# Nine odd merge gates computed in a stage of their own, four pairs of them by seven products, in a hybrid encoder layer

## The reference, cut to what matters

```python
h = rms_norm(x, pre_g); u = h @ w_in          # 1024 tokens x 1024
...                                           # ya, yb, yc: three attention branches, 1024 x 512 each
gates = jax.nn.sigmoid(mg).reshape(b, s, 3, D_MODEL)      # mg: the last 3*1024 columns of u
m = gates[:, :, 0] * (ya @ wa) + gates[:, :, 1] * (yb @ wb) + gates[:, :, 2] * (yc @ wc)
x = x + rms_norm(m @ w_out, post_g)
x = x + jax.nn.sigmoid(x @ w_pg) * (p_i @ w_pe)
```

## Time and profile before

| what | value |
|---|---|
| median of 3 runs | 1332.03 us (1331.99 to 1332.58) |
| the profiled execution: span from first to last instruction | 1330.3 us |
| the runs' median less that span (what lies around it) | 1.7 us |
| PE busy | 1312.1 us, 99% |
| DVE, ACT, POOL busy | 680.8, 575.5, 352.0 us |
| DMA | 72.18 MB, mean 54 GB/s |
| the chain that ended last | PE 90%, DVE 4%, ACT 3% |

### The profile page before, as it was taken

One profiled execution on the slowest core, in us unless ns is written; L12 is line 12 of the kernel. 1 busy time (PEld: TensorE's weight loads), 2 busy tenths in 40 slices (PEclk: granted clock), 3 DMA queues, 4 the chain that ended last, 5 costly groups with the idle time before them and its releaser, 6 DMA issues.

```text
span 1330.3 us, 17488 instructions
## 1 busy us (share of the span) xinstructions
PE 1312.1 (99%) x6636; PEld 1072.0 (81%) x6636; DVE 680.8 (51%) x1285; ACT 575.5 (43%) x1106; POOL 352.0 (26%) x239
## 2 busy tenths in 40 slices
PE   8999999999999999999999999999999999999998
PEld 6788877888888778788888888888877888888887
DVE  6354655556522677786633435555557337435222
ACT  6355455553222577676422245555554223223210
POOL 4122212222434311130244512221211443213100
PEclk9999999999999999999999999999999999999999
DMA  6111112111111200000111211111001114422111
GB/s 214 63 41 41 46 36 57 52 32 52 49 48 32 67 30 16 17 20 21 52 52 32 81 61 33 51 51 42 32 24 41 48 40 167 140 81 70 58 40 40
DMA packets 25712, 72.18 MB, mean 54 GB/s; under 512 B 2808, under 2 KB 4728, under 8 KB 25504
## 3 DMA queue, kind: packets, MB, share of 16 engines
q1 hardware_dynamic: 25632, 71.09, 16.9%
HBM read 66.86 MB, written 4.23 MB: 53 GB/s over the span
## 4 chain that ended last, share of the span: by engine, by line
PE 90%; DVE 4%; ACT 3%; issue 1%; DMA 1%; POOL 1%; SPq 0%; ACTq 0%; DVEq 0%; POOLq 0%
PE ps L934 18%; PE ps L953 14%; PE ps L1290 13%; PE ps L1548 7%; PE ps L1528 6%; PE ps L1175 5%; PE ps L1342 5%; PE ps L1331 2%; PE ps L973 2%; PE ps L1112 2%; PE ps L1028 2%; PE ps L1260 2%; PE ps L1554 2%; PE ps L1406 2%; PE ps L1143 1%; PE ps L1234 1%
## 5 line engine op out<-in xcount | busy, mean ns | idle before, releaser
L728 POOL TENSOR_TENSOR w_lo<-stage,w_hi 128x1024 fp32r<-128x1024 f32 (+2 forms) x84 | 190.3, 2265 | 577.5 <-ACT w_hi L1598 577.5
L1598 ACT CAST w_hi<-stage 128x1024 fp32r<-128x1024 f32 (+2 forms) x92 | 91.3, 992 | 198.0 <-PE ps L934 125.9
L2148 DVE TENSOR_TENSOR pt_lo<-ps,pt_hi 128x512 fp32r<-128x512 f32 (+2 forms) x160 | 97.1, 607 | 80.6 <-ACT pt_hi L1962 40.3
L953 PE MATMUL ps<-h_hi,w_hi 128*128 128x512 f32 x272 | 110.3, 405 | 0.0
L934 PE MATMUL ps<-h_hi,w_hi 128*128 128x512 f32 x352 | 108.9, 391 | 0.7 <-POOL w_lo L728 0.7
L934 PE MATMUL ps<-h_lo,w_hi 128*128 128x512 f32 x352 | 108.5, 389 | 0.0
L934 PE MATMUL ps<-h_hi,w_lo 128*128 128x512 f32 x352 | 108.4, 389 | 0.0
L1290 PE MATMUL ps<-h_hi,w_hi 128*128 128x512 f32 x256 | 106.8, 417 | 0.0
L953 PE MATMUL ps<-h_hi,w_lo 128*128 128x512 f32 x272 | 106.2, 391 | 0.0
L953 PE MATMUL ps<-h_lo,w_hi 128*128 128x512 f32 x272 | 106.1, 390 | 0.0
L1290 PE MATMUL ps<-h_hi,w_lo 128*128 128x512 f32 x256 | 100.5, 392 | 0.0
(11 more groups left out here) (386 smaller groups left out, 3059.3 us busy)
## 6 DMA issues: line engine op xcount, KB each, us to landing
stage<-in_w_gates SPq DMA_DIRECT2D x24, 512.0 KB, 3.6
stage<-in_w_qkvg_a SPq DMA_DIRECT2D x19, 512.0 KB, 4.4
stage<-in_w_qkvg_c SPq DMA_DIRECT2D x16, 512.0 KB, 3.6
m<-in_x_tok SPq DMA_DIRECT2D x8, 512.0 KB, 6.4
stage<-in_w_branch SPq DMA_DIRECT2D x8, 512.0 KB, 3.7
y_plain<-in_x_tok SPq DMA_DIRECT2D x8, 512.0 KB, 3.7
stage<-in_w_pg SPq DMA_DIRECT2D x16, 256.0 KB, 3.0
out<-y_plain SPq DMA_DIRECT2D x16, 256.0 KB, 2.0
```

The lines of the kernel that those rows point to most:

```text
L728: nc.gpsimd.tensor_tensor(dst, stage[:, staged, 0:width], f32(hi), ALU.subtract).then_inc(w_ready, 1)
L953: done = mm(ps[:, half_bank(T), :], w[:, slot, k * P:(k + 1) * P], h[:, k, g * SEQ:(g + 1) * SEQ], start=k == 0 and part == 0, stop=k == K ...
L1598: nc.scalar.copy(dst, stage[:, staged, 0:width]).then_inc(w_hi_done, 1)
L2148: sub = lambda out, whole, hi: nc.vector.tensor_tensor(out, whole, f32(hi), ALU.subtract)
```

## The change

Of the 24 gates the nine with f odd and at least 3 are taken out of the merges (gates 3, 5, 7 of each). They are computed right behind the first q and k, when h is ready. Gate (b=0, f=3) is plain (`plain_gate`, 24 matmuls for each group); the other eight go in four pairs J, each by seven products of 12 matmuls (`gate_product`). Pairs of gates are products of h by two weight blocks, so the state quarters and their sums are the same for all J and are formed once: POOL and DVE add hi and lo back together (four quarters of 128x2048), DVE forms four sums, ACT casts and DVE splits them. For each J, DVE forms four sums of weights and makes all the low parts, DVE does seven adds on PSUM, ACT takes tanh and SP stores each 128x512 quarter to DRAM (`gate_scratch`). In the merges SP reads the finished rows back into `s_row(1)` (`load_gate_row`).

In a merge PE now runs: gate 0, gate 1, branch 0, branch 1, gate 2, then for each pair: pair_first, pair_rest, gate 2p+2 (the gate of the pair behind it). In merge 2 both gates 4 and 6 stand behind pair 1, and branch 6 follows pair 2 directly. ACT, POOL, DVE and SP follow that order; numbers of weight blocks (`N_MERGE`, `N_B`, ...) and slots shift.

```diff
+GATE_PLAIN = (0, 3)
+GATE_PAIRS = [((0, 5), (0, 7)), ((1, 3), (1, 5)), ((1, 7), (2, 3)), ((2, 5), (2, 7))]
...
             def merge_gate(b, f, n, slot, c):
 
-                pe.wait_ge(mg_tanh, LEAD + b * KC + f - 1)
+                if c:
+                    pe.wait_ge(merged, LEAD + b * KC + 2)
+                else:
+                    pe.wait_ge(mg_tanh, LEAD + gate_tanhs(b, f - 2))
                 project(n, slot, gate_bank(b, c))
...
             def merge_rest(b):
 
-                n, slot = N_MERGE[b], N_MERGE[b] % 2
-                merge_gate(b, 2, n + 3, 1 - slot, 0)
-                merge_branch(b, 1, n + 4, slot)
-                merge_gate(b, 3, n + 5, 1 - slot, 1)
+                n = N_MERGE[b]
+                merge_branch(b, 1, n + 3, (n + 1) % 2)
+                merge_gate(b, 2, n + 4, n % 2, 0)
                 for p in PAIRS[b]:
...
+                    pair_first(b, p, at, at % 2)
+                    pair_rest(b, p, at + 1, 1 - at % 2)
+                    for c, number in enumerate(gates_behind(b, p)):
+                        merge_gate(b, 2 * p + 2 + 2 * c, number, number % 2, c)
                 if KC // 2 - 1 not in PAIRS[b]:
-                    merge_branch(b, 6, n + 14, slot)
-                    merge_branch(b, 7, n + 15, 1 - slot)
+                    merge_branch(b, 6, n + 11, (n + 11) % 2)
+                    merge_branch(b, 7, n + 12, (n + 12) % 2, count=2)
...
+            plain_gate(0)
             first_product("q", 1, range(KC))
             first_product("k", 1, range(KC))
+            plain_gate(1)
+            for J in range(N_PAIRS):
+                for product in range(7):
+                    gate_product(J, product)
+            pe.wait_ge(g_added, 7 * N_PAIRS - 4)
             half_step(-2, lambda T: None)
...
+            def gate_product(J, product):
...
+                gate_bank_free(7 * J + product)
+                if product == P1:
+                    pe.wait_ge(gw_ready, 4 * J + 2)
+                elif product == P3:
+                    pe.wait_ge(gw_ready, 4 * J + 3)
+                elif product == P7:
+                    pe.wait_ge(gw_ready, 4 * J + 4)
+                if J == 0 and product >= P6:
+                    pe.wait_ge(gt_ready, T_LO.index(state) + 1)
...
+            pool.wait_ge(h_ready, LEAD + QT)
+            for T, half in ((1, 0), (4, 1)):
+                hi, lo = h_quarter(half, 0)
+                nc.gpsimd.tensor_tensor(G_SUM[T], f32(hi), f32(lo), ALU.add).then_inc(gt_whole, 1)
```

More of the change, by code:

```diff
@@ new lines, in merge_rest, with plain_gate @@
+                if KC // 2 - 1 not in PAIRS[b]:
+                    merge_branch(b, 6, n + 11, (n + 11) % 2)
+                    merge_branch(b, 7, n + 12, (n + 12) % 2, count=2)
+            def plain_gate(g):
+                hi, lo = G_PLAIN
+                pe.wait_ge(gp_ready, 1)
+                if g == 0:
+                    pe.wait_ge(h_ready, LEAD + 6)
+                bank = [0, 3][g]
+                for k in range(KC):
+                    for part, (w, h) in enumerate([(hi, h_hi), (hi, h_lo), (lo, h_hi)]):
+                        done = mm(ps[:, bank, :], w[:, k * P:(k + 1) * P], h[:, k, g * SEQ:(g + 1) * SEQ],
+                                  start=k == 0 and part == 0, stop=k == KC - 1 and part == 2)
+                done.then_inc(gate_half, 1)
@@ new lines, in gate_product @@
+            def gate_product(J, product):
+                a, a22 = G_A1, G_A22[J % 2]
+                (s2s4, s3s1) = G_S
+                (hi, lo), first, state = {P1: (a, 0, "11"), P2: (a, SEQ, "21"), P3: (s2s4, SEQ, "22"), P6: (s2s4, 0, 2),
+                                          P7: (s3s1, 0, 3), P5: (s3s1, SEQ, 1), P4: (a22, 0, 4)}[product]
+                gate_bank_free(7 * J + product)
+                if product == P1:
+                    pe.wait_ge(gw_ready, 4 * J + 2)
[5 more added lines that the diff above has]
+                    pe.wait_ge(gt_ready, T_LO.index(state) + 1)
+                for c in range(QT):
+                    cols = slice(first + c * P, first + (c + 1) * P)
+                    for part, (w, h) in enumerate([(hi, 0), (hi, 1), (lo, 0)]):
+                        done = mm(ps[:, g_bank(J, product), :], w[:, cols], G_STATE[state][h][:, c, :],
+                                  start=c == 0 and part == 0, stop=c == QT - 1 and part == 2)
+                done.then_inc(g_done, 1)
@@ new lines, in merge, with plain_gate_hi @@
+                    split(n + 11, width=512)
+                    beside(range(2, 4))
+                    split(n + 12, width=512, count=2)
+                    act.wait_ge(block_done, LEAD + n + 9)
+                    act.wait_ge(merged, LEAD + b * KC + 5)
+                    nc.scalar.activation(s_row(0), banks(gate_bank(b, 1)), ACT.Tanh, scale=0.5).then_inc(mg_tanh, 1)
+            def plain_gate_hi():
+                act.wait_ge(gp_in, 16)
+                nc.scalar.copy(G_PLAIN[0], stage[:, 0, :]).then_inc(gw_hi_done, 1)
@@ L2383, in merge @@
                     state_lo(j)
[L2384 removed]
+                merge_add(b, 1, n + 3, 1)
                 state_lo(3)
```

569 lines of the change are left out of this document (409 added, 160 removed).

## The result

| | before | changed |
|---|---|---|
| median of 12 runs | 1332.08 us | 1335.63 us |
| ratio, 95% interval | | 1.0024 (1.0016 to 1.0032) |
| span of the profiled execution | 1330.3 us | 1334.4 us |

The changed kernel is slower: by 0.24% in the ratio, which is estimated from all runs, and by 3.6 us (0.27%) between the medians. The prediction had 6.8 us more, 1338.8, and a range of 1331.5 to 1346.0: the sign, the range and the places are right, the size is twice what came.

What follows compares the result with a forecast made beforehand. PE's matmul count times start spacing was taken as the bound. Terms -10.9 - 0.5 + 2.7 + 0.4 + 3.5 + 3.5 + 6.5 + 2.0 - 0.4 = +6.8 on 1332.0 gave 1338.8 us, range 1331.5 to 1346.0.

Steps and rivals of the forecast that it cites:

- 48 matmuls fewer: Four gate pairs on PE, each 84 matmuls instead of 96, at 0.2268 us each: -10.9 us.
- start and the new stage: Plain gate 0 fills PE's wait before group 1's q, -0.5; P3 of the first pair waits for DVE, +2.7.
- merge 0: Start of merge 0, where merge_add is one operation: PE waits +0.4 us (0 to 0.8).
- merge 1's pair 1: PE waits for POOL's and DVE's chains before pair 1 and in pair_rest: +3.5 us (0 to 4.9).
- merge 2's pair 1: Same chain as in merge 1, before pair 1 and in pair_rest: +3.5 us.
- branch 6's wait: End of pair 2 in merge 2: PE waits for DVE's last addition to m, +6.5 us (5.9 to 7.2).
- clock: After the idle time before branch 6, matmuls start 0.43 us apart for 4.3 us: +2.0 us (0 to 4.1).
- output projection: DVE has its time for q_lo during the last branch, so PE's wait goes: -0.4 us.
- the start of each merge: PE waits before pair 1 and in pair_rest: +3.5 us each in merges 1 and 2, +0.4 in merge 0.
- P3's stall: New stage, first gate pair: P3 wanted at 61.1, its operand ready at 63.8, +2.7 us (0 to 6.7).
- the merges' stalls don't come: Rival, chance 0.17: POOL gets its ports between DVE's operations, pair 1 ready in time; 1329.2 at its edge, 1334 with half the stalls.
- The faster rival: Rival, chance 0.10: nothing binds at branch 6, so the tail and clock losses go; 1323 to 1330 us.

Runs made afterwards that it cites:

- the early cast's experiment: Changed kernel with ACT's cast of pair 1's weights moved ahead of its wait for the state sums: 1333.81 us, ratio 1.0010.
- 3.7 for both: Changed kernel with pair 1's weights cast ahead of the state sums and its first product waiting for one merged block, not two: 1331.94 us, ratio 1.0000.
- the 11 executions: Changed kernel with branch 6 of merge 2 waiting for five merged blocks instead of six: 1333.24 us, ratio 1.0002.

## Why the prediction was right or wrong

| term | predicted | measured |
|---|---|---|
| 48 matmuls fewer | -10.9 | -10.9 (336 products in 78.04 us with a wait of 1.8; 336 x 0.2268 = 76.2) |
| start and the new stage | -0.5 + 2.7 = +2.2 | +0.2 + 1.2 = +1.4 |
| merge 0 | +0.4 | +1.0 |
| merge 1's pair 1 | +3.5 | +2.3 |
| merge 2's pair 1 | +3.5 | +2.3 |
| branch 6's wait | +6.5 | +6.4 (idle 6.2 and a slower restart) |
| clock | +2.0 | +2.6 |
| output projection | -0.4 | -0.9 |
| sum | +6.8 | +4.1 in the profile, +3.6 in the runs |

Merge 2's measured 11.1 us are these 2.3, 6.4 and 2.6, less 0.2 of rounding and of small waits.

**Right:** what bounds the kernel, what the matmuls give, and the largest loss. The wait of branch 6 was laid out from the earlier trace rows to a tenth of a us, and moving the gate back took it away. The fall of the clock came with the idle time, and the matmuls in the gap showed that it was the clock. Its size, +2.0, lies in what five profiles show (1.7 to 3.0), with luck: the prediction took from the tail of the kernel that the clock falls 4.4 us after PE stops, and the runs show 2.0 to 4.8. That the merges' stalls are too short to bring it on came true (no profile has a half clock there), but not because they are shorter than 4.4 us: in the start it fell behind idle times of 1.8 and 2.3 us, and behind 3.6 us, by the mean clocks, most likely in about half of the executions.

**Wrong in size:** the step "the start of each merge", +3.5 us for merge 1 and again for merge 2, each measured as +2.3. It makes the forecast of 6.8 us twice what came. The prediction took 1.8 us for the first wait and 1.7 for what follows in pair_rest, and the profile shows 1.5 and 0.8 (the 42 matmuls of the pair took 10.31 us, where 9.52 is usual). The copy of the first product on ACT was counted as 0.4 to 2.3 us of its own on top of the wait for the 128x768 split; the two run side by side (the copy ends at 727.6, the split at 728.2), and the later of them is all that PE sees. Of the 0.8, 0.3 stand in front of the first product of pair_rest; most of the rest is in four single starts of 0.31 to 0.34 us instead of 0.227, whose cause is not shown. Twice 1.2 us is 2.4 of the 2.7 us between the sum and the profile. The rest is small: P3's stall was 1.8 where 2.7 was taken, mainly because the exclusion held DVE up for 4.7 us, not 5.6; the clock cost 0.6 more than said, the slow stretch having been 5.3 us long where the start of the kernel had shown 4.3; a 0.6 us idle time in front of branch B's first weights, which gate 7 of merge 0 had covered, had not been looked for; and the output projection gained 0.5 more. The runs then show half a us less than the profiled execution, which took 1336.23 us where the median is 1335.63.

**The rivals.** The one in which the merges' stalls don't come fell: they came. Its argument (POOL gets its turn between DVE's operations) was half true, as POOL was done 11.1 us after the state sums, where 11.7 was laid out. The faster rival needed branch 6's wait not to bind, and it bound in full. That two chains, POOL's and DVE's, end within 1 us of each other before pair 1 stood in the prediction's working (both at about 665.9), and it is what decided the early cast's experiment; its theory of 4 us went by POOL's chain alone, and its rival by both.

## What to carry to other kernels

Saving matmuls pays only if the order that goes with it keeps as much PE work behind each DVE or POOL tail as the tail is long: here a 10.9 us gate stood over a 6.4 us tail, and taking it away cost 9 us with the clock, nearly all that the saved matmuls gave. Before moving a block, list what it covered; after a stall of several us count the slow clock behind it as well. Where two chains end together in front of a wait, shorten both, or expect little (1.8 us here for the one, 3.7 for both, 1.0 of it in the profile the clock's).

## What the runs showed of the hardware beyond what was expected

- PE idle for 6.2 us, in five profiled kernels: the granted clock fell to 0.50 between 2.0 and 4.8 us after PE had stopped and was full again 3.4 to 6.0 us after it had gone on, 1.7 to 3.0 us lost. Behind 3.6 us it stayed at 1.00 in the profiled execution, while six of the 11 executions have a mean clock as low as the changed kernel's. In the start of two profiled executions it fell behind idle times of 1.8 and 2.3 us. So a single profile shows neither how long an idle time is safe nor what one costs. Filling the gap with 24 matmuls that nobody reads made the kernel 1.7 us faster in the runs.
- Two POOL sums of 128x2048 beside two of DVE took 12.2 and 9.2 us; DVE by itself does all four in 9.7.
